# Tables, state matrices, modulation sums and convolution taps at other places in a written engine order

## The chip, the cores and the metric

The kernel runs on one core of one Trainium2 chip. The metric is the device time of one execution in microseconds (us); the figure for the kernel before is the median of three runs.

## The reference, cut to what is computed

Two token streams of 128 tokens and width 1024 (a prompt and a sample) pass through the same two layers. Every layer has three branches (a convolution of 31 taps, a state space model run in both directions, and attention), which are merged by gates and added to the stream. All arithmetic is float32.

```python
def _layer(x, mods, lp, angles, ctx_k, ctx_v, init_re, init_im):
    shift, scale, gate = mods                       # _adaln(c, w_ada, b_ada): silu(c) @ w + b
    h = _rmsnorm(x, lp['norm_g']) * (1.0 + scale) + shift
    z = h @ lp['w_in']
    conv_in, conv_gate, ssm_in, ssm_gate, q, k, v, attn_gate, merge = jnp.split(z, cuts, axis=-1)
    ya = _conformer_conv(conv_in, ...)              # a*sigmoid(g), 31 taps, layer norm, silu
    br_a = (ya * jax.nn.silu(conv_gate)) @ lp['w_conv_out']
    yb, fin_re, fin_im = _s5_bidirectional(ssm_in, ...)
    yg_a, yg_b = jnp.split(jax.nn.gelu(yb) @ lp['w_ssm_glu'], 2, axis=-1)
    br_b = (yg_a * jax.nn.sigmoid(yg_b) * jax.nn.silu(ssm_gate)) @ lp['w_ssm_out']
    ...
    br_c = (_blocked_attention(q, k_all, v_all) * jax.nn.silu(attn_gate)) @ lp['w_attn_out']
    mixed = g_a * br_a + g_b * br_b + g_c * br_c
    return x + gate * (mixed @ lp['w_out']), side
```

In the state space model `lam_bar = exp(lam*dt)`, `b_bar = ((lam_bar-1)/lam) * b`, and the state follows `h[t] = lam_bar*h[t-1] + b_bar u[t]` per group (32 groups, 64 complex states, 16 channels).

## The kernel before, in words

**One order, five engines.** `stages()` and `order(l)` (L56 and L126) write out one list of stages. Every engine walks the same list and does its own share of each stage, waiting on semaphores; so the place of a stage in the list sets what an engine does before and after it, and an instruction that waits holds up all that stands behind it on its engine. SyncE (SP) issues the weight loads in the list's order into seven slots (`raw`, `RAW` = 7, 512 KB each), and a slot is loaded again when its slab has been read.

**Split products.** The units `cg`, `ssm`, `ca` (L40) and all merge (`me`), branch (`br`) and output (`wo`) products are done as three products of rounded parts (L826 to L828). For each piece of weights (two k tiles) ScalarE writes the high part (`high_parts`, L1163) into one of a few rooms (five `early_room`, three `late_room`), and VectorE subtracts it for the low part (`low_parts`, L1466). TensorE waits for the low part (L821). `ahead(l, u, beside)` (L446) says how many pieces of the next unit are split beside a unit's own, two as a rule. The other units (`q`, `kv`, `sg`, `ag`, `gg`, `glub`, `glua`) are plain float32 products (L798).

**The opening.** The layer norm, the modulation (`ada`, `adaE`, `adaT`) and `hT` give the scaled input; `early` splits it. `tabA`, `tabS`, `tabB`, `tabC` make the tables of powers of lam (VectorE, with ScalarE for `tabS`). `bT` and `cT` transpose the state matrices b and c. `pre` (L1759) multiplies b by powers of lam in halves of 16 groups, six VectorE operations each, into the one buffer `pre`; `preE` transposes it on TensorE (`states_in`, L834) and ScalarE copies it to `E`. `pre` of the second half waits until the first has been transposed (L1764). `bbar` (L1746) scales b itself.

**The state space part.** `pack` and `UT` bring the tokens into groups (`Uz`). `S` (L938) multiplies E by Uz: eight banks of four products, each bank copied by ScalarE (partitions 0 to 63, L1342) and VectorE (64 to 127, L1743) into `H`. In the kernel before, the product writes its bank with the chunk number outermost, so both copies read the bank in a row and write runs of 16 values. `cp` (L1780) needs tA and tB and, here, `bbar`; `bz` on GpSimd needs `bbar`; `K` on TensorE needs `cp` and `bz`. `scan` runs 32 steps of four VectorE operations, `qkn` normalises q and k, `Y` reads the states back (`HY`, L1409 on ScalarE and L1881 on VectorE).

**Convolution taps.** A layer has 124 tap operations on VectorE (L1570), dealt out by hand: 4 ahead of `Y`, 18 in it, 25 in `att` 0, 20 in `att` 1, 14 beside each of the two B combinations, and the rest (29) in `("conv", -1, "C0")`, behind which `cback` waits.

**End of a layer.** `comb` A mixes the last branch; `pre` of the next layer stands as a block between; `wout` multiplies by w_out, `wx` (`out_and_add`, L1588) adds to x; `sq` and `xn` normalise for the next layer.

Side banks in PSUM are a ring of three, claimed in the list's order (`Ring`, L211).

## Time and profile before

| | kernel before |
|---|---|
| median of three runs (lowest to highest) | 738.4 us (738.39 to 740.62) |
| the profiled execution: time, and its span from first to last instruction | 741.45 us, 739.4 us |
| mean granted TensorE clock in that span | 0.962 |
| busy: TensorE, VectorE, ScalarE, GpSimd | 656.6, 546.4, 291.3, 35.4 us |
| weight loads | 16 DMA engines busy about half of the span, 117.65 MB |

The span is what the rows below count in, from its first instruction; the time is 2.05 us longer than the span, and the profiled execution is 3.05 us above the median. A row of the timeline gives start, duration, engine, line, operation, tile written and tiles read, how often, and in brackets the idle time of the engine ahead of it and what ended it. A granted clock of 1.00 is 2.4 GHz, 0.50 is 1.2 GHz.

### The profile page before, as it was taken

Reading aid. Unit: us, or ns where it says so; the run is one execution under the profiler, and the core shown is the slowest. Engines: PE = TensorE matmul, PEld = TensorE weight load, DVE = VectorE, ACT = ScalarE, POOL = GpSimd, SP = SyncE. Lnnn points to the kernel's source line nnn. Section 1 sums busy time; section 2 is a strip of 40 time slices with the busy share of each in tenths; the row PEclk is TensorE's granted clock in tenths of the full one; section 3 lists DMA queues with packets and bytes.
Section 4 is the critical chain, followed back from the end, with each engine's and each line's share of the span. In section 5 each row is a group of like instructions: output and inputs, shape, how many; then the busy total and the mean of one; then the engine's idle time right before and its main releaser. Section 6 shows DMA issues by size and latency. Waiting matters only on the chain.

```text
span 739.4 us, 9579 instructions
## 1 busy us (share of the span) xinstructions
PE 656.6 (89%) x3573; PEld 473.0 (64%) x3573; DVE 546.4 (74%) x1024; ACT 291.3 (39%) x454; POOL 35.4 (5%) x49
## 2 busy tenths in 40 slices
PE   3669679999898999987898797999898999989997
PEld 1357574653744688775787686665485568867885
DVE  3873769994757988988767444899778699897564
ACT  2454322211535454442544642311254345434541
POOL 2100010102000000010000001001200000000000
PEclk9979789999999999998999998999999999999999
DMA  8973623862675365544433347281254236655531
GB/s 283 355 204 97 204 71 118 281 225 57 208 230 173 100 218 165 176 132 124 144 122 105 113 150 274 81 293 54 55 195 121 81 95 194 189 153 151 192 121 57
DMA packets 67305, 117.65 MB, mean 159 GB/s; under 512 B 11052, under 2 KB 15484, under 8 KB 67260
## 3 DMA queue, kind: packets, MB, share of 16 engines
q1 hardware_dynamic: 66980, 116.94, 49.8%
q8 instruction: 28, 0.46, 0.3%
q14 instruction: 17, 0.14, 0.1%
q10 hardware_dynamic: 280, 0.11, 0.1%
HBM read 112.51 MB, written 1.38 MB: 154 GB/s over the span
## 4 chain that ended last, share of the span: by engine, by line
PE 71%; DVE 20%; issue 3%; ACT 3%; SPq 1%; DMA 0%; POOL 0%; ACTq 0%; POOLq 0%; DVEq 0%
PE proj L798 20%; PE proj L826 11%; PE proj L827 11%; PE proj L828 11%; DVE cvacc L1570 4%; PE side L813 3%; DVE raw_split L1463 3%; PE side L951 3%; PE side L965 2%; PE side L1044 2%; PE long L768 2%; PE side L994 2%; DVE tA L1463 1%; DVE tB L1463 1%; PE side L1042 1%
## 5 line engine op out<-in xcount | busy, mean ns | idle before, releaser
L798 PE MATMUL proj<-raw,hT 128*128 128x512 f32 (+1 forms) x320 | 132.0, 558 | 0.0
L1570 DVE SCALAR_TENSOR_TENSOR cvacc<-cvpad,taps,cvacc 128x256 f32<-128x256 f32 x240 | 99.2, 478 | 0.3
L798 PEld LDWEIGHTS proj<-raw,hT 128*128 128x128 f32 x320 | 58.2, 190 | 58.8 <-issue 57.0
L1179 ACT ACTIVATE wide_split<-raw 128x1024 fp32r<-128x1024 f32 x56 | 58.6, 1059 | 58.0 <-PE proj L828 53.2
L1463 DVE TENSOR_TENSOR raw_split<-raw,wide_split 128x1024 fp32r<-128x1024 f32 x56 | 67.6, 1220 | 18.6 <-ACT wide_split L1179 17.6
L827 PE MATMUL proj<-raw_split,H_split 128*128 128x512 f32 x192 | 76.6, 399 | 0.0
L826 PE MATMUL proj<-wide_split,H_split 128*128 128x512 f32 x144 | 59.4, 412 | 12.8 <-DVE raw_split L1463 12.5
L828 PE MATMUL proj<-wide_split,H_split 128*128 128x512 f32 x144 | 58.0, 403 | 0.0
L1463 DVE TENSOR_TENSOR raw_split<-raw,utok_split 128x1024 fp32r<-128x1024 f32 x28 | 34.2, 1221 | 12.6 <-ACT utok_split L1179 12.5
L1179 ACT ACTIVATE utok_split<-raw 128x1024 fp32r<-128x1024 f32 x28 | 29.6, 1058 | 35.1 <-PE proj L828 35.1
L827 PEld LDWEIGHTS proj<-raw_split,H_split 128*128 128x128 f32 x192 | 37.2, 194 | 7.3
L826 PEld LDWEIGHTS proj<-wide_split,H_split 128*128 128x128 f32 x144 | 27.9, 193 | 21.1 <-DVE raw_split L1463 13.1
L1463 DVE TENSOR_TENSOR H<-H,qkt 128x128 f32<-128x128 f32 x128 | 38.4, 300 | 2.2
L827 PE MATMUL proj<-raw_split,mixed_split 128*128 128x512 f32 x96 | 39.1, 407 | 0.0
L827 PE MATMUL proj<-raw_split,qM_split 128*128 128x512 f32 x96 | 37.7, 393 | 0.0
L828 PEld LDWEIGHTS proj<-wide_split,H_split 128*128 128x128 f32 x144 | 28.1, 195 | 6.3
L813 PE MATMUL side<-ident,pre 128*128 128x128 f32 x128 | 19.9, 293 | 11.0 <-DVE pre L1463 7.5
L798 PE MATMUL proj<-raw,HY 128*128 128x512 f32 x64 | 29.0, 596 | 0.0
L1376 ACT ACTIVATE pre<-side,nmx 128x128 f32<-128x128 f32 (+1 forms) x32 | 13.2, 416 | 39.7 <-PE side L813 16.4
L1152 ACT ACTIVATE gates<-proj 128x512 f32<-128x512 f32 x12 | 7.0, 597 | 54.7 <-PE proj L798 54.7
L951 PE MATMUL side<-Uz,EC 128*128 128x128 f32 x128 | 20.5, 340 | 8.9 <-DVE Uz L1736 8.9
L813 PEld LDWEIGHTS side<-ident,pre 128*128 128x128 f32 x128 | 16.6, 152 | 18.1 <-DVE pre L1463 7.7
(251 smaller groups left out, 1336.9 us busy)
## 6 DMA issues: line engine op xcount, KB each, us to landing
raw<-in_w_in SPq DMA_DIRECT2D x104, 512.0 KB, 4.2
raw<-in_w_ada SPq DMA_DIRECT2D x48, 512.0 KB, 5.1
...
```

The source lines that it names most:

```text
L768: m = T.matmul(ring.bank(part)[rows_, 0:ADA_W], cond[:, kt, :], w[:, j // 2, ADA_W * (j % 2):ADA_W * (j % 2) + ADA_W], start=(kt == 0), st ...
L798: m = T.matmul(proj.bank((l, u, s))[:, 0:n], lhs[:, s, kt, :], w[:, i, :], start=(kt == 0), stop=last)
L813: return T.transpose(out, in_, ident[0:k, 0:k])
L826: T.matmul(bank[:, :], hi, whi, start=(kt == 0), stop=False)
L827: T.matmul(bank[:, :], hi, wlo, start=False, stop=False)
L828: m = T.matmul(bank[:, :], lo, whi, start=False, stop=last)
L951: m = T.matmul(out[:, gg, r, :, :, :], E[:, r, gp, :], Uz[:, 2 * gp:2 * gp + 2, :].rearrange("p a (s k) -> p a s k", s=NS), start=True, st ...
L965: m = T.matmul(side.bank(key)[0:48, 80 * b:80 * b + 80], bz[:, r, g % 16, :], CP[:, r, :, g, :], start=(r == 0), stop=(r == 1))
L994: T.matmul(side.bank(key)[:, 0:2 * nk * P], qT[:, s, p, :], kz[s][:, :, :].rearrange("p a k -> p (a k)"), start=True, stop=True).then_inc( ...
L1179: S.activation(piece_room[m], piece_raw(m), ACT.Copy).then_inc(piece_hi, 1)
L1463: return V.tensor_tensor(out, a, b, op)
L1570: m = V.scalar_tensor_tensor(acc, src, taps[:, t, j:j + 1], acc, ALU.mult, ALU.add)
```

## The change

- The opening of layer 0: `tabB` moves from ahead of `early` to behind the unit `cg`; `cT` moves ahead of the unit `ssm`, and c is loaded right behind b; the first `preE` moves behind `ca` and the taps. `pre` of the second half goes to a buffer of its own (`first_pre`, in the room of `H` that held `xn`), so it no longer waits for the first half's transposes. `cg` now splits four pieces of `ssm` beside its own.
- `bbar`: in layer 0 behind `cp`, in layer 1 between `ssm` and `ca` (before: ahead of `UT` in both).
- `S`: the products write the bank with the chunk number innermost, the copies read the bank in a row and write single values 512 bytes apart.
- `adaT` (modulation sums) behind `Y`; `qkT` 1 ahead of `att` 0; taps dealt out anew: 16 or 8 ahead of `Y` (layer 0, 1), 40 or 30 in `att` 0, 22 in `att` 1, 12 beside each B combination, so 4 or 22 remain for `C0`.
- `pre` of layer 1, first half, behind the transposes of branch A, and both halves with low parts of the A units between their six operations (`upto`).
- The edge of the layers: the three low parts of the next `cg` behind the first `wx`; `preE` of the second half cut in two on ScalarE with `sq` between; the first `hT` transposes inside the last product of w_out (`tokens_t`); the second `wx` behind the first `early`.

```diff
+TAPS_IN_ZONE = (16, 8)
+TAPS_IN_ATT = (((8, 8, 8, 8, 8), (7, 4, 4, 7, 0)), ((6, 6, 6, 6, 6), (7, 4, 4, 7, 0)))
...
-    begin = [("unit", "cg"), ("tabC",), ("bT", 0), ("unit", "ssm"), ("cT", 0), ("pre", 0, 0), ("preE", 0, 0),
-             ("chunks", "ca", 4), ("pre", 0, 1), ("unit", "ca"), ("taps", 0), ("pack",), ("preE", 0, 1)]
+    begin = [("unit", "cg"), ("tabB",), ("tabC",), ("bT", 0), ("cT", 0), ("unit", "ssm"), ("pre", 0, 0),
+             ("chunks", "ca", 4), ("pre", 0, 1), ("unit", "ca"), ("taps", 0), ("preE", 0, 0), ("pack",), ("preE", 0, 1)]
     if l:
-        begin = [("hT", 0, 0), ("hT", 1, 0), ("early", 0, 0), ("sq", l, 1), ("early", 1, 0), ("xn", l, 1),
+        begin = [("hT", 0, 0), ("hT", 1, 0), ("early", 0, 0), ("wx", l - 1, 1), ("early", 1, 0), ("sq", l, 1), ("xn", l, 1),
-                 ("unit", "ca"), ("pack",)]
+                 ("bbar", l), ("unit", "ca"), ("pack",)]
+    turn = [] if l else [("bbar", l)]
     return (begin
-            + [("bbar", l), ("bz", 0), ("UT",), ("S",), ("cp",), ("convT", 0), ("convT", 1), ("unit", "q"), ("unit", "kv"),
+            + [("UT",), ("S",), ("cp",)] + turn + [("bz", 0), ("convT", 0), ("convT", 1), ("unit", "q"), ("unit", "kv"),
-            + [("scan", 0, NCHUNK), ("qkn",), ("adaT", l, 2)] + nxt("adaT", n, 0)
-            + [("conv", 4, None), ("Y",), ("qkT", 0), ("att", 0)] + nxt("adaE", n, 1)
-            + [("geT",), ("qkT", 1), ("att", 1), ("unit", "glub"), ("unit", "glua"), ("split", 0), ("split", 1)]
+            + [("scan", 0, NCHUNK), ("qkn",), ("conv", TAPS_IN_ZONE[l], None), ("Y",), ("adaT", l, 2)] + nxt("adaT", n, 0)
+            + [("qkT", 0), ("qkT", 1), ("att", 0)] + nxt("adaE", n, 1)
+            + [("geT",), ("att", 1), ("unit", "glub"), ("unit", "glua"), ("split", 0), ("split", 1)]
-            + [("brT", "B", 0), ("brT", "B", 1), ("conv", 14, "B0"), ("comb", "B", 0)]
-            + nxt("bT", n) + [("brT", "C", 0), ("brT", "C", 1), ("conv", 14, "B1"), ("comb", "B", 1)]
+            + [("brT", "B", 0), ("brT", "B", 1), ("conv", 12, "B0"), ("comb", "B", 0)]
+            + nxt("bT", n) + [("brT", "C", 0), ("brT", "C", 1), ("conv", 12, "B1"), ("comb", "B", 1)]
-            + nxt("taps", n) + [("cback", 0), ("cback", 1), ("comb", "C", 1)] + nxt("pre", n, 0)
-            + [("brT", "A", 0), ("brT", "A", 1), ("comb", "A", 0)] + nxt("preE", n, 0) + nxt("pre", n, 1)
-            + [("comb", "A", 1), ("wout", 0), ("wout", 1), ("wx", 0)] + nxt("sq", n, 0) + nxt("preE", n, 1)
-            + nxt("xn", n, 0) + [("wx", 1)])
+            + nxt("taps", n) + [("cback", 0), ("cback", 1), ("comb", "C", 1)]
+            + [("brT", "A", 0), ("brT", "A", 1)] + nxt("pre", n, 0) + [("comb", "A", 0)] + nxt("preE", n, 0)
+            + nxt("pre", n, 1) + [("comb", "A", 1), ("wout", 0), ("wout", 1), ("wx", l, 0)] + nxt("preE", n, 1)
+            + nxt("sq", n, 0) + nxt("preF", n, 1) + (nxt("xn", n, 0) or [("wx", l, 1)]))
...
-                            ("tabS",), ("hT", 0, 0), ("hT", 0, 1), ("tabB",), ("early", 0, 0), ("early", 0, 1),
+                            ("tabS",), ("hT", 0, 0), ("hT", 0, 1), ("early", 0, 0), ("early", 0, 1),
...
+        first_pre = H[:, :, :].rearrange("p a b -> p (a b)")[:, 0:2048].rearrange("p (r g j c) -> p r g j c", r=2, g=16, j=L)
+        pre_of = lambda ll, half: first_pre if (ll, half) == (0, 1) else pre
...
+                    sp.wait_ge(bbar_done, l)
...
+                    c_loads(0)
-                    c_loads(0)
...
+            def tokens_t(l, h, s):
+                pe.wait_ge(xn_second if h else xn_first, ls(l, s))
+                key = ("hT", l, h, s)
+                side.claim(pe, key)
+                for i in range(4):
+                    d = 4 * h + i
+                    m = transpose(side.bank(key)[:, P * i:P * i + P], xn[:, s, P * d:P * d + P])
+                m.then_inc(side.full, 1)
...
-                                          pre[:, r, g:g + 2, :, :].rearrange("p g j c -> p (g j c)"))
+                                          pre_of(ll, half)[:, r, g:g + 2, :, :].rearrange("p g j c -> p (g j c)"))
...
-                    pe.wait_ge(xn_second if h else xn_first, ls(l, s))
-                    key = ("hT", l, h, s)
-                    side.claim(pe, key)
-                    for i in range(4):
-                        d = 4 * h + i
-                        m = transpose(side.bank(key)[:, P * i:P * i + P], xn[:, s, P * d:P * d + P])
-                    m.then_inc(side.full, 1)
+                    if l == 0 or s:
+                        tokens_t(l, h, s)
...
-                        out = side.bank(key)[:, :].rearrange("p (k g a r s) -> p g r a s k", k=NCHUNK, g=2, a=2, r=2)
+                        out = side.bank(key)[:, :].rearrange("p (g a r q) -> p g r a q", g=2, a=2, r=2)
-                                m = T.matmul(out[:, gg, r, :, :, :], E[:, r, gp, :],
-                                             Uz[:, 2 * gp:2 * gp + 2, :].rearrange("p a (s k) -> p a s k", s=NS),
+                                m = T.matmul(out[:, gg, r, :, :], E[:, r, gp, :], Uz[:, 2 * gp:2 * gp + 2, :],
...
+                                    if s == 1 and kt == 5 and l + 1 < DEPTH:
+                                        for h in range(2):
+                                            tokens_t(l + 1, h, 0)
...
-                elif k == "preE":
+                elif k in ("preE", "preF"):
-                    for r in range(2):
+                    for r in ((0,) if stg == ("preE", l + 1, 1) else (1,) if k == "preF" else range(2)):
...
-                    high_parts(ahead(l, "cg"))
+                    high_parts(ahead(l, "cg", 4))
...
-                        S.activation(H[0:64, 1:NCHUNK + 1, 16 * i:16 * i + 16],
-                                     side.bank(key)[0:64, :].rearrange("p (k x) -> p k x", k=NCHUNK),
+                        dst = H[0:64, 1:NCHUNK + 1, 16 * i:16 * i + 16].rearrange("p k x -> p x k")
+                        S.activation(dst, side.bank(key)[0:64, :].rearrange("p (x k) -> p x k", k=NCHUNK),
...
-                    low_parts(ahead(l, stg[1]))
+                    low_parts(ahead(l, stg[1], 4 if stg[1] == "cg" else 2))
...
-                        V.tensor_copy(H[64:128, 1:NCHUNK + 1, 16 * i:16 * i + 16][:, ::-1, :],
-                                      side.bank(key)[64:128, :].rearrange("p (k x) -> p k x", k=NCHUNK)
+                        dst = H[64:128, 1:NCHUNK + 1, 16 * i:16 * i + 16][:, ::-1, :].rearrange("p k x -> p x k")
+                        V.tensor_copy(dst, side.bank(key)[64:128, :].rearrange("p (x k) -> p x k", k=NCHUNK)
                 elif k == "bbar":
+                    if ll == 0:
+                        dve.wait_ge(cp_done, 2)
...
-                    side.filled(dve, ("E", ll, 3) if half else ("cT", ll, 1))
+                    if half == 0:
+                        side.filled(dve, ("cT", ll, 1))
+                    elif ll:
+                        side.filled(dve, ("E", ll, 3))
+                    else:
+                        for h, s in itertools.product(range(2), range(NS)):
+                            side.filled(dve, ("hT", ll, h, s))
+                        dve.wait_ge(pre_done, 1)
+                    upto = lambda i: low_parts(piece_at[(l, f"meA{half}", 0)] + i) if ll else None
+                        upto(3 * r + 1)
+                        upto(3 * r + 2)
+                        upto(3 * r + 3)
-                        m = tt_(pre[:, r, :, :, :], t1, t2, ALU.add if r else ALU.subtract)
+                        m = tt_(pre_of(ll, half)[:, r, :, :, :], t1, t2, ALU.add if r else ALU.subtract)
...
-                    dve.wait_ge(bbar_done, l + 1)
+                    if l:
+                        dve.wait_ge(bbar_done, l + 1)
...
-                        else:
-                            for _ in range(5):
-                                conv_tap(*taps_left.pop(0))
+                        for _ in range(TAPS_IN_ATT[l][s][p]):
+                            conv_tap(*taps_left.pop(0))
...
+                        low_parts(piece_at[(l, "wo1", 3)] + 1)
+                elif k == "wx":
+                    out_and_add(stg[1], 1, stg[2])
+                    if stg[2] == 0:
-                elif k == "wx":
-                    out_and_add(l, 1, stg[1])

```

## Rows read from the trace of the kernel before

**Rows 1.** Page, part 1: busy us, share of the span and instructions, by engine.

```profile
PE 656.6 (89%) x3573; PEld 473.0 (64%) x3573; DVE 546.4 (74%) x1024; ACT 291.3 (39%) x454; POOL 35.4 (5%) x49
```

**Rows 2.** TensorE's waits: engine, line waited for: us in all, times, longest us.

```profile
PE proj L826 <- DVE raw_split L1463: 22.3, 10, 8.4
...
PE side L813 <- DVE cvacc L1570: 2.5, 2, 1.8
```

**Rows 3.** Windows: stretch, length, busy us (count) by engine, clock, DMA share, GB/s.

```profile
42.80:48.00 5.20, 5.19 (x13) 4.11 (x14) 5.01 (x5) 2.92 (x4) 0.00 (x0) 0.51 0.36 133
...
48.00:56.00 8.00, 8.00 (x36) 6.53 (x35) 4.41 (x13) 2.54 (x3) 0.00 (x0) 1.00 0.91 219
...
103.20:108.70 5.50, 5.48 (x26) 5.50 (x27) 1.39 (x2) 1.18 (x2) 1.85 (x4) 0.50 0.00 0
```

**Rows 4.** Timeline of the opening: sums' transposes, sums, first split product.

```profile
33.10 0.44 PE L813 MATMUL side<-ident,adarow 128*128 128x128 f32 x2 [0.51 <-ACT adarow L1202]
...
37.77 0.23 DVE L1463 TENSOR_TENSOR ada<-side,modc 128x8 f32<-128x8 f32 x2
...
42.81 0.77 PE L826 MATMUL proj<-gates_split,mixed_split 128*128 128x512 f32 x1 [8.41 <-DVE raw_split L1463]
```

**Rows 5.** Windows: tabB, tabC, pre half, bbar, cp, scan with qkn, S to Y.

```profile
29.27:36.55 7.28, 4.50 (x54) 2.19 (x42) 6.56 (x23) 2.90 (x7) 0.00 (x0) 1.00 0.93 327
...
50.47:53.80 3.33, 3.33 (x16) 2.69 (x16) 3.26 (x13) 0.12 (x1) 0.00 (x0) 1.00 1.25 279
...
72.62:79.91 7.29, 0.00 (x0) 0.00 (x0) 7.17 (x6) 0.61 (x2) 0.00 (x0) 0.67 0.43 143
...
97.96:101.79 3.83, 1.09 (x16) 0.96 (x16) 3.79 (x6) 1.77 (x4) 0.00 (x0) 1.00 0.18 70
...
114.25:128.75 14.50, 14.50 (x55) 5.69 (x54) 14.25 (x12) 1.81 (x4) 0.00 (x0) 1.00 0.43 135
...
128.76:176.33 47.57, 47.57 (x303) 26.05 (x302) 42.41 (x144) 8.79 (x26) 7.49 (x7) 1.00 0.65 216
...
113.49:183.66 70.17, 70.17 (x394) 35.10 (x392) 57.37 (x156) 12.46 (x32) 7.49 (x7) 1.00 0.55 179
```

**Rows 6.** Copies by line: ns min/median/max, first and last start, form.

```profile
L1342 ACT ACTIVATE H<-side x16: 591/591/592, 105.3 to 468.5; 64x512 f32<-64x512 f32 x16
...
L1743 DVE COPY H<-side x16: 694/695/696, 105.3 to 468.5; 64x512 f32<-64x512 f32 x16
...
L1229 ACT ACTIVATE bbar<-side x4: 1032/1051/1054, 58.6 to 275.6; 128x512 f32<-128x512 f32 x4
...
L1881 DVE COPY HY<-H x8: 1023/1048/1070, 186.6 to 544.2; 64x1024 f32<-64x1024 f32 x8
```

**Rows 7.** Timeline ahead of S in layer 0.

```profile
79.95 3.68 PE L813 MATMUL side<-ident,pre 128*128 128x128 f32 x16 [7.46 <-DVE pre L1463]
...
93.56 1.23 DVE L1463 TENSOR_TENSOR pre<-tA,tB 128x1024 f32<-128x1024 f32 x1
...
103.22 10.28 PE L951 MATMUL side<-Uz,EC 128*128 128x128 f32 x64 [4.16 <-DVE Uz L1736]
```

**Rows 8.** Timeline at the start of attention of stream 1, layer 0.

```profile
225.01 2.06 DVE L1570 SCALAR_TENSOR_TENSOR cvacc<-cvpad,taps,cvacc 128x256 f32<-128x256 f32 x5
...
229.20 1.10 PE L994 MATMUL side<-kz,qM 128*128 128x512 f32 x2 [1.82 <-DVE kz L1830]
```

**Rows 9.** Timeline at the start of Y in layer 0.

```profile
184.07 3.78 ACT L1409 ACTIVATE HY<-H 64x1024 f32<-64x1024 f32 x2
...
187.78 0.43 PE L1042 MATMUL side<-qM,Uz 128*64 128x64 f32 x2 [3.12 <-DVE HY L1881]
```

**Rows 10.** Timeline in the A combination of layer 0.

```profile
347.10 0.80 PE L826 MATMUL proj<-wide_split,H_split 128*128 128x512 f32 x1 [5.09 <-DVE raw_split L1463]
```

**Rows 11.** Timeline at the edge of the layers.

```profile
417.83 0.47 PE L826 MATMUL proj<-gates_split,mixed_split 128*128 128x512 f32 x1 [2.69 <-issue]
```

**Rows 12.** Timeline at the start of S in layer 1.

```profile
458.25 2.05 PE L951 MATMUL side<-Uz,EC 128*128 128x128 f32 x8 [4.76 <-DVE Uz L1736]
```

## The prediction, made before the changed kernel was run

> **What bounds the kernel now.** I read the page first: TensorE is busy 656.6 of 739.4 us [rows 1], so all that a new order can win is its 82.8 us of idling and what the clock costs beside it. Then TensorE's waits: VectorE ends most of them, the low parts of split weights alone ten waits of 22.3 us, the last taps of a layer two of 2.5 [rows 2]. Then the windows around such waits: after the wait ahead of 42.8 the granted clock is 0.51 (the 1.2 GHz level) and 13 products take 5.2 us, then it is 1.00 and 36 take 8.0, so a product is 0.40 or 0.23 us; the bank products of S begin at 0.50 as well [rows 3]. I count nine waits with such a stretch behind or around them. So TensorE is the bound nearly everywhere, and the question at each moved stage is whether VectorE still ends a wait there.
>
> **The opening of layer 0.** The modulation sums run on VectorE at 37.77, though TensorE's transposes for them are done at 33.54; the first split product starts at 42.81 after a wait of 8.41 [rows 4]. In between VectorE does `tabB`, to 36.55 [rows 5]. With `tabB` gone the sums move up by 4.2, and with them the second half of `hT`, `early` and the first low part: first product at about 38.8. Then I follow VectorE. TensorE reads the first `cg` piece (12 products, cold, 5.2) until 44.0 and the third until 49.5 (24 more at 0.23); only then the fourth `ssm` piece has a room. ScalarE's copy of 1024 columns, from its 0.59 for 512 [rows 6], is 1.1, and a low part costs VectorE what one of the six equal operations of a half of `pre` costs (7.29/6 = 1.2 [rows 5]): ready at 51.9. Behind it stand on VectorE `tabB` 7.28, `tabC` 3.33, four low parts of `ca` 4.8, two halves of `pre` 14.6 [rows 5], together 30.0, without a wait among them that I can find: 81.9. TensorE meanwhile has `cg` to 52, some 5 for b and c and 48 products each of `ssm` and `ca` at 0.23, so until about 79, and the wait of 7.46 for `pre` [rows 7] goes and VectorE is late by some 3 only at the end. From the last `pre` (94.79) to the first product of S (103.22) it took 8.4 [rows 7]; 3.8 of that was `bbar` [rows 5], now behind `cp`. The copy of `pack` comes into that line, as it now stands on ScalarE behind the first `preE`; 0 to 1.9, I take 0.8. S then starts at 81.9 + 8.4 - 3.8 + 0.8 = 87.3 instead of 103.2: **-15.9**. Bounds: -17 without the `pack`, -8 if some link of this chain of thirty steps costs twice what it should. On SP the four loads of c now pass three `ssm` loads; those pieces wait for rooms, which covers some 3 us of delay.
>
> **The copies of S.** ScalarE will write values 512 bytes apart. Its nearest row, 512 columns written 64 bytes apart, takes 1.05 us against 0.59 for the copy of now; VectorE's nearest row, 1024 values read 512 bytes apart, takes 1.05 us, no more per value than its S copy of now with 0.695 for 512 [rows 6]. So I take 1.05 on ScalarE and 0.7 on VectorE, with 1.25 (VectorE by ScalarE's factor 1.8) as the other bound and no gain possible on either. With three banks TensorE isn't held by 1.05; **+1.0** for both layers.
>
> Here the Trainium skill has a rule that speaks against the change: "Advanced Engine Details and Errata", SBUF Cachelines, says that accesses which go to another 16-byte line each time pay. For ScalarE the rows agree, for VectorE's reads they don't. By that rule VectorE's copies pay as well, the second rival below.
>
> **Scan to Y, layer 0.** VectorE becomes the bound. From the end of S (113.49) it needs about 0.7 to its last copy, 14.5 for `cp`, now 3.8 for `bbar`, 47.6 for scan and `qkn` [rows 5], 16 taps at 0.41 (five in 2.06 [rows 8]) and 1.05 for the first `HY`: 74.2. Now `Y` starts at 187.78, which is 74.3, after `adaT` had held VectorE [rows 9]. TensorE is done after 70.2 [rows 5] and ScalarE's `HY` some 2 later (two copies in 3.78 [rows 9]), so the wait stays: **-0.1**. In layer 1 (`bbar` earlier, 8 taps) the same sum ends at ScalarE's `HY`, about 0.6 early. GpSimd's `bz` waits for `bbar` but ends some 5 us before `K` needs it.
>
> **Attention.** `qkT` 1 goes ahead, so the 1.82 ahead of the first scores of stream 1 [rows 8] loses the cause that its row names; but these scores also wait until VectorE has read the sums of stream 0, and in front of that stand in layer 0 eight taps twice instead of five, 6 x 0.41 = 2.4 more. With `adaT` and `qkT` 1 ahead of the scores (1.5) and the `kz` copy saved, stream 1 starts 3.0 late; in stream 1 taps and slack cancel: **+3.0**. In layer 1 (six instead of five, one sum less) it is +0.6, which cancels the 0.6 above: **0**.
>
> **C combination.** Layer 0 has 4 taps left there instead of 29, so VectorE is 10 us ahead and the waits for the last taps and the low part behind them (2.6 together, in [rows 2]) go but for 0.5: **-2.1**. Layer 1 has 22 instead of 29, 2.9 less: of three waits of 4.5 there, 1.8 + 1.8 go: **-3.6**. The taps that filled this went to stages where, up to the two costs above, VectorE idled.
>
> **A combination.** TensorE waits 5.09 at 347.10 because the whole first `pre` (7.3) stands in front of a low part [rows 10]; a second such wait, for the second half, is 2.4 long. With low parts between the operations each costs 1.2 + 1.2 = 2.4, less than the 12 x 0.23 = 2.8 that TensorE takes for a piece. The lookahead ends inside the first three operations, so 1.5 of the first wait stays: 3.6 + 2.4 = **-6.0**. Bound -3: the first half misses its slot.
>
> **The edge.** The first product of layer 1 waits until 417.83, the last 2.69 for `hT` [rows 11]. With three low parts (3.6) behind `wx` x is ready 3.6 earlier, `sq` no longer holds `E` copies, and the transposes run inside the last product. The first product comes almost 5 earlier, but then the second stream's `hT` waits for the second `wx`, now behind `early`: I take **-2.9**, between 0 and -5.9 (both waits gone).
>
> **S, layer 1.** `bbar` leaves the line, its 3.8 of the wait of 4.76 [rows 12]: **-3.7**. VectorE idles between `ssm` and `ca`, where it goes.
>
> **Clock.** Where waits go, the stretches at 1.2 GHz behind them go: up to 2.7 us each for the two S stages (half of 5.5 [rows 3]), and, as half of the stretches that the granted clock shows, 4.4 in A (5.1 and 3.7 us) and 1.9 in C (3.8 us): 11.7. As waits of 1 to 4 us stay or come anew ahead of S, `Y` and stream 1, I take 7, less 0.9 for a longer wait ahead of `Y`: **-6.1**; bounds 0 and -11.
>
> **Sum.** -15.9 + 1.0 - 0.1 + 3.0 - 2.1 - 3.6 - 6.0 - 2.9 - 3.7 - 6.1 = -36.4 us on the profiled 741.45 (span 739.4, 2.05 around it), so 705.0 in such an execution. That one lay 3.05 above the median 738.4, so the forecast for a median is **702.0**. Its own range is 694 to 710 (the clock's bounds and some 3 us of the opening).
>
> **The rivals.**
> - The copies of S cost VectorE 1.25 each. Eight copies then take 4.4 longer, of which S's own pace hides some 1.5, and as VectorE sets the start of `Y` in both layers, 2.9 each come onto the path, and 1.1 each on S: 702 + 8 = **710**. For it: ScalarE's row. Against it: VectorE's strided reads. This is the result that the Trainium skill's rule on 16-byte lines ("Advanced Engine Details and Errata", SBUF Cachelines) would give.
> - The opening gives half: VectorE's chain of thirty steps meets a wait (the fourth `ssm` piece, for which VectorE waits ahead of all tables), so S starts at 95 instead of 87: 702 + 8, and some 6 more when the first half in A also misses its slot: **716**. For it: nothing on VectorE can pass a late low part. Against: no other link shows a wait.
> - Clock and edge give their full bounds: 702 - 5 - 3 = **694**.
> - Slower than before: the single-value writes into `H` stop being a rate of one value per cycle on VectorE, and its chain through S, `cp` and scan, which has no slack in either layer, takes it all. 16 copies must add 36.4 + 2.2 us, so it decides from 2.4 us more per copy, 3.1 instead of 0.7; at 3.5 each the time is **747**. ScalarE's factor of 1.8 is far below that, no row has more.
> - The change doesn't do what it says: tables moved behind `cg` just stall later. With the opening at 0 and the rest kept: **718**.
>
> **How the numbers follow.** Forecast 0.55; copies 0.18; half an opening 0.12; full bounds 0.06; nothing in the opening 0.03; slower 0.04; no change, by several of these at once, 0.02. The range takes the forecast's own band, the copies and half an opening: 692 to 719. A difference of 0.3% (2.2 us) is about what a measurement of this kernel can tell from no change. Faster 0.94, same 0.02, slower 0.04.
>
> **What the changed profile would show.** The first split product near 38.8; S near 87, with no `bbar` ahead of it; VectorE's S copies at 0.7 and ScalarE's near 1.05; `Y` 74 us behind the end of S, with VectorE as releaser; scores of stream 1 late behind the taps; no wait above 2 us in the A combination; the start of layer 1 some 3 us sooner behind the last product of w_out; S of layer 1 within 1.2 us of the transposes of U. I am wrong if VectorE's copies take over 1 us, if S starts after 92, or if waits of 3 us and more appear where none were.

## The result and the profile after

The changed kernel takes 714.4 us (median of four, 713.0 to 715.4) beside 738.8 for the kernel before on the same chip: a ratio of 0.966, 95% interval 0.964 to 0.969, so 24.4 us faster. Compared once more with the kernel before, it took 713.1 beside 739.6 (0.963, 0.960 to 0.966). The forecast was 702.0 with a range of 692 to 719: the direction and the range held, the gain was two thirds of what was forecast. The profiled execution after took 713.04 with a span of 711.0; the one before took 741.45 with 739.4. Trace against trace 28.4 us went.

The page after: busy times by engine, and the granted TensorE clock in 40 slices.

```profile
PE 652.4 (92%) x3573; PEld 466.5 (66%) x3573; DVE 551.5 (78%) x1024; ACT 297.3 (42%) x454; POOL 36.4 (5%) x49
...
PEclk9989889998998999999999999999998999999999
```

TensorE is busy 4.2 us less than in [rows 1], in a span 28.4 shorter: what went is mostly its idling (82.8 us before, 58.6 now). The waits of TensorE after, as who waited for whom: total, times, longest.

```profile
PE proj L833 <- DVE raw_split L1477: 11.3, 10, 4.2
PE side L1053 <- DVE HY L1908: 8.4, 2, 5.4
...
PE side L1005 <- DVE qkt L1477: 4.5, 2, 2.7
...
PE long L1022 <- DVE pre L1882: 2.9, 2, 1.7
...
PE side L820 <- DVE taps L1629: 2.0, 1, 2.0
```

The low parts cost 11.3 where they cost 22.3 in [rows 2], and the waits for the last taps are gone from the list. What stands out now are the waits ahead of Y (HY), two kinds in the attention (qkt, pre) and one for the copy of the taps.

Where the 28.4 us lie, by the start of the same instruction in both traces (the starts of before that the prediction used are in [rows 4, 7 to 9, 11, 12], the rest is read from its trace in the same way):

| stage | before | after | change | forecast |
|---|---|---|---|---|
| start to S, layer 0 | 103.2 | 90.1 | -13.1 | -15.9 |
| S, layer 0 | 10.3 | 9.1 | -1.2 | in copies and clock |
| end of S to Y, layer 0 | 74.3 | 75.7 | +1.4 | -0.1 |
| Y to the first split product behind the attention, layer 0 | 67.3 | 72.0 | +4.7 | +3.0 |
| from there to the transposes of cvacc | 56.2 | 56.9 | +0.7 | 0 |
| C combination, layer 0 | 21.5 | 19.4 | -2.1 | -2.1 |
| A combination, layer 0 | 54.6 | 44.6 | -10.0 | -6.0 and clock |
| w_out and edge to S, layer 1 | 70.9 | 64.6 | -6.3 | -6.6 |
| S, layer 1 | 10.3 | 7.4 | -2.9 | in copies and clock |
| end of S to Y, layer 1 | 67.6 | 67.5 | -0.1 | 0 |
| Y to the first split product, layer 1 | 63.6 | 66.7 | +3.1 | 0 |
| the rest | 139.7 | 137.0 | -2.7 | -3.6 |
| copies of S, clock, over all stages | | | in the rows above | +1.0, -6.1 |
| sum | | | -28.4 | -36.4 |

Three places carry the miss. First the opening. TensorE after, from the first transposes of `pre` that wait to S (start, duration, tile, count, wait and what ended it):

```profile
82.18 1.09 PE L820 MATMUL side<-ident,pre 128*128 128x128 f32 x8 [1.99 <-DVE taps L1629]
...
86.28 1.11 PE L820 MATMUL side<-ident,H 128*128 128x128 f32 x4 [0.77 <-ACT EC L1258]
...
90.12 9.10 PE L963 MATMUL side<-Uz,EC 128*128 128x128 f32 x64 [0.83 <-DVE Uz L1750]
```

VectorE in the same stretch:

```profile
79.50 1.22 DVE L1477 TENSOR_TENSOR H<-tA,tB 128x1024 f32<-128x1024 f32 x1
80.65 1.28 DVE L1740 SCALAR_TENSOR_TENSOR mixed<-th,proj 128x512 f32<-128x512 f32 x2
81.84 0.28 DVE L1629 COPY taps<-side 128x128 f32<-128x128 f32 x1
```

VectorE's chain ended at 80.7, even before the forecast 81.9. But eight transposes of the first half of `pre`, which VectorE had finished at 71.3, stood behind the copy of the taps, whose bank they want, and VectorE reached that copy only behind everything else.

Then the attentions. TensorE after, ahead of stream 1 in layers 0 and 1:

```profile
214.59 0.66 PE L1022 MATMUL long<-v,pre 128*128 128x64 f32 x4 [1.20 <-DVE pre L1882]
...
218.80 2.04 PE L1005 MATMUL side<-kz,qM 128*128 128x512 f32 x2 [2.67 <-DVE qkt L1477]
220.64 4.99 PE L805 MATMUL proj<-raw,HY 128*128 128x512 f32 x8
...
541.91 0.66 PE L1022 MATMUL long<-v,pre 128*128 128x64 f32 x4 [1.71 <-DVE pre L1882]
...
545.32 2.05 PE L1005 MATMUL side<-kz,qM 128*128 128x512 f32 x2 [1.87 <-DVE qkt L1477]
547.16 5.56 PE L805 MATMUL proj<-raw,HY 128*128 128x512 f32 x8
```

In layer 0 a late start was forecast: the two waits are 3.87 together where they were 1.98 before. In layer 1 they are 3.58 where they were 3.13, so there the terms nearly cancelled, as forecast. Not foreseen was what stands behind them in both layers: two scores take 2.04 and 2.05, the eight products with `HY` 4.99 and 5.56. In the trace of before they took 1.10 and 3.60 in both layers. Layer 1 of before:

```profile
569.82 0.66 PE L1011 MATMUL long<-v,pre 128*128 128x64 f32 x4 [1.31 <-DVE pre L1854]
...
573.87 1.10 PE L994 MATMUL side<-kz,qM 128*128 128x512 f32 x2 [1.82 <-DVE kz L1830]
574.80 3.60 PE L798 MATMUL proj<-raw,HY 128*128 128x512 f32 x8
```

The windows after show the granted clock of those stretches (the column behind POOL's):

```profile
219.00:225.00 6.00, 6.00 (x9) 2.48 (x10) 3.89 (x10) 2.30 (x5) 0.00 (x0) 0.63 0.19 47
...
545.30:551.00 5.70, 5.68 (x7) 2.51 (x8) 3.98 (x10) 2.30 (x5) 0.00 (x0) 0.50 0.00 1
```

The third place is the start of Y, where TensorE waits 5.44 us in layer 0, and the miss of 1.5 there.

### The profile page after: what moved, and what is told of

The parts are those of the page before. It is cut to its first block and busy times, and to the rows that moved or that the text cites. A ratio compares the mean times of both kernels' runs of the same rounds, so it can differ in the third digit from the quotient of the medians.

```text
span 711.0 us, 9584 instructions
## 1 busy us (share of the span) xinstructions
PE 652.4 (92%) x3573; PEld 466.5 (66%) x3573; DVE 551.5 (78%) x1024; ACT 297.3 (42%) x454; POOL 36.4 (5%) x49
## 5 line engine op out<-in xcount | busy, mean ns | idle before, releaser
L1477 DVE TENSOR_TENSOR raw_split<-raw,wide_split 128x1024 fp32r<-128x1024 f32 x56 | 67.9, 1220 | 21.6 <-ACT wide_split L1193 20.9
L1193 ACT ACTIVATE wide_split<-raw 128x1024 fp32r<-128x1024 f32 x56 | 58.6, 1059 | 55.9 <-PE proj L835 55.9
L833 PE MATMUL proj<-wide_split,H_split 128*128 128x512 f32 x144 | 57.9, 402 | 4.7 <-DVE raw_split L1477 4.7
L835 PE MATMUL proj<-wide_split,H_split 128*128 128x512 f32 x144 | 56.9, 395 | 0.0
L834 PEld LDWEIGHTS proj<-raw_split,H_split 128*128 128x128 f32 x192 | 36.4, 190 | 7.3
L834 PE MATMUL proj<-raw_split,mixed_split 128*128 128x512 f32 x96 | 38.5, 401 | 0.0
L805 PE MATMUL proj<-raw,HY 128*128 128x512 f32 x64 | 32.4, 653 | 0.0
L1053 PE MATMUL side<-qM,Uz 128*64 128x64 f32 x128 | 19.7, 239 | 8.4 <-DVE HY L1908 8.4
L1055 PE MATMUL side<-EC,HY 128*64 128x64 f32 x256 | 25.4, 237 | 0.0
L834 PE MATMUL proj<-raw_split,HY_split 128*128 128x512 f32 x64 | 24.9, 390 | 0.0
```

The source lines that it names most:

```text
L805: m = T.matmul(proj.bank((l, u, s))[:, 0:n], lhs[:, s, kt, :], w[:, i, :], start=(kt == 0), stop=last)
L833: T.matmul(bank[:, :], hi, whi, start=(kt == 0), stop=False)
L834: T.matmul(bank[:, :], hi, wlo, start=False, stop=False)
L835: m = T.matmul(bank[:, :], lo, whi, start=False, stop=last)
L1053: T.matmul(o, Uz[:, g, :], M[:, :, g // 2, :], start=True, stop=False)
L1055: m = T.matmul(o, HY[:, q % 2, gi, r, :, :].rearrange("p s k -> p (s k)"), CP[:, r, 1:L + 1, g, :], start=False, stop=(r == 1))
```

## The experiments

Each kernel is the changed one with the edit shown, if nothing else is said. Times are medians of four, ratios are to the kernel before on the same chip, and traces are compared with that of the changed kernel (span 711.0).

| kernel | us | ratio, 95% interval | span of the trace |
|---|---|---|---|
| changed | 714.4 | 0.966 (0.964 to 0.969) | 711.0 |
| changed, once more | 713.1 | 0.963 (0.960 to 0.966) | 711.3 |
| S in the layout of before | 712.0 | 0.962 (0.961 to 0.964) | 710.5 |
| attention taps dealt anew | 707.1 | 0.954 (0.949 to 0.958) | 704.7 |
| no taps ahead of Y | 711.9 | 0.960 (0.957 to 0.964) | 709.9 |
| copy of the taps later | 711.1 | 0.961 (0.959 to 0.962) | 708.7 |
| tables back | 714.9 | 0.965 (0.962 to 0.968) | 713.0 |
| pre in one piece | 722.0 | 0.975 (0.971 to 0.978) | 720.7 |
| edge back | 719.6 | 0.972 (0.968 to 0.976) | 716.6 |
| all taps dealt as before | 704.6 | 0.953 (0.951 to 0.954) | 703.3 |
| bbar back ahead of S | 714.5 | 0.966 (0.964 to 0.968) | 711.1 |
| combined | 692.8 | 0.936 (0.931 to 0.942) | 692.4 |
| combined, HY early | 692.2 | 0.936 (0.935 to 0.938) | 688.5 |

### The measure: the changed kernel once more

> The changed kernel once more, nothing altered, on the chip and beside the runs of the other three. It is the measure for small differences. Theory: its stages differ from the first trace of it only where the granted clock fell or did not fall behind the same waits (S of layer 0, the start of Y, the first split products of layer 0), so 713 to 716, and each stage without such a stretch within 0.2 us. Rival: the first profiled execution (713.0) was a different case from the others, with other waits.

713.1 us, the same waits at the same places: 5.47 ahead of Y, 1.20 and 2.66, 1.70 and 1.88 ahead of stream 1. Stage by stage the traces differ by up to 0.3 us, and by 0.5 ahead of S of layer 0 and 0.4 in it (9.51 against 9.10). So a stage of one trace is good to some 0.3 us where the clock is steady. The start of S in layer 0 scatters more: in the eight traces here whose order is the same up to there it lies between 89.6 and 91.0. The two medians of this kernel differ by 1.2 us; differences of less than 2 us are read below from the traces, not from the medians.

### The copies of S

```diff
-    out = side.bank(key)[:, :].rearrange("p (g a r q) -> p g r a q", g=2, a=2, r=2)
+    out = side.bank(key)[:, :].rearrange("p (k g a r s) -> p g r a s k", k=NCHUNK, g=2, a=2, r=2)
...
-    dst = H[64:128, 1:NCHUNK + 1, 16 * i:16 * i + 16][:, ::-1, :].rearrange("p k x -> p x k")
-    V.tensor_copy(dst, side.bank(key)[64:128, :].rearrange("p (x k) -> p x k", k=NCHUNK)
+    V.tensor_copy(H[64:128, 1:NCHUNK + 1, 16 * i:16 * i + 16][:, ::-1, :],
+                  side.bank(key)[64:128, :].rearrange("p (k x) -> p k x", k=NCHUNK)
```

> The changed kernel with the S stage alone back in the layout of before (chunk outermost). In the changed kernel's trace VectorE's eight copies of S follow one another at 0.92 us with no idle time, in the kernel before they took 0.69 and stood 0.89 apart, which is TensorE's own rate for a bank at full clock. Theory: the new layout costs 0.22 us a copy, and as TensorE needs 0.89 a bank anyway, only about 0.25 us of each S stage and 0.25 of each last copy reach the path: this kernel is 1 us faster than the changed one (time 713.4 against 714.4, the profile's S of layer 1 7.1 long against 7.38, Y of layer 0 starting 0.5 sooner behind the start of S). Rival: the layout shortened S (10.26 to 9.1 and 7.4 us in the two layers), so taking it back costs 1 to 3 us a layer, up to 720.

VectorE's copies of S, first in the changed kernel, then in this one (shortest, median, longest in ns):

```profile
L1758 DVE COPY H<-side x16: 1031/1048/1053, 92.2 to 439.9; 64x512 f32<-64x512 f32 x16
```

```profile
L1758 DVE COPY H<-side x16: 694/695/696, 92.5 to 439.5; 64x512 f32<-64x512 f32 x16
```

A copy takes 1.05 us on VectorE, not 0.7, and as long on ScalarE. But in either layout the copies of S in layer 1 start 0.89 apart, which is TensorE's pace for a bank at full clock; the longer ones overlap. So S of layer 1 takes 7.38 us in either layout, and from its start to VectorE's last copy it is 8.49 against 8.11: the layout costs 0.4 us a layer, all of it in the last copy. The theory was right on the size (0.8 for both layers, 1.0 expected), but not on its place, as S itself was to fall to 7.1. The rival, that the layout had shortened S, fell: with the layout of before S of layer 1 takes 7.38 here, so the 10.3 of before were its low clock.

### The attention's taps

```diff
-TAPS_IN_ATT = (((8, 8, 8, 8, 8), (7, 4, 4, 7, 0)), ((6, 6, 6, 6, 6), (7, 4, 4, 7, 0)))
+TAPS_IN_ATT = (((9, 9, 9, 4, 3), (11, 4, 4, 7, 0)), ((7, 7, 8, 2, 1), (11, 4, 4, 7, 0)))
```

> The changed kernel with the taps of the attention dealt in another way: stream 0 gets 9,9,9,4,3 instead of 8,8,8,8,8 (layer 0) and 7,7,8,2,1 instead of 6,6,6,6,6 (layer 1), stream 1 gets 11,4,4,7,0 instead of 7,4,4,7,0, the rest (none in layer 0, one tap in layer 1) goes to the C combination. Theory: the taps of the last two steps hold the copy of the probabilities and the sums of stream 0, so the waits of 1.20 and 2.67 us (layer 0) and 1.71 and 1.87 (layer 1) ahead of stream 1 go but for 0.3 each, and with them the granted clock's fall behind them: the first piece with HY takes 3.6 us again instead of 4.99 and 5.56, the first scores 1.1 instead of 2.05, and the first split products of layer 0 gain 1.5. Together some 12 us, 702 us. Rival: VectorE is the bound of the whole attention, so the same taps make the same waits at other steps: 0 to 3 us, 711 to 714. Second rival: the clock's fall has nothing to do with these waits but with the transposes of q and k that no longer stand there: waits gone, clock still low, 707.

TensorE in this kernel, ahead of stream 1 of layer 0:

```profile
216.70 1.10 PE L1005 MATMUL side<-kz,qM 128*128 128x512 f32 x2 [0.69 <-DVE qkt L1477]
217.63 3.60 PE L805 MATMUL proj<-raw,HY 128*128 128x512 f32 x8
```

The wait is 0.69 instead of 2.67, the other is gone, and scores and products are back at 1.10 and 3.60. The same in layer 1 (0.35, 1.10). With the transposes of q and k still moved, the clock stays up once the taps no longer hold VectorE, so the second rival, in which those transposes alone bring the clock down, falls. From Y to the first split product it is 67.6 and 61.7 instead of 72.0 and 66.7. The expected 12 us were not all there, though: VectorE, now later at the end of stream 1, makes TensorE wait 0.89 and 0.52 for its last copy of the probabilities, the first split products of layer 0 run at a granted clock of 0.60 and those of layer 1 at 0.75, and in the C combination of layer 1, with one tap more, a wait grows from 1.28 to 1.69. Of 12 us 7 came (6.3 by the trace).

### The taps ahead of Y

```diff
-TAPS_IN_ZONE = (16, 8)
+TAPS_IN_ZONE = (0, 0)
...
-            + [("brT", "B", 0), ("brT", "B", 1), ("conv", 12, "B0"), ("comb", "B", 0)]
+            + [("brT", "B", 0), ("brT", "B", 1), ("conv", 14, "B0"), ("comb", "B", 0)]
```

(and 14 for B1.)

> The changed kernel without the 16 (layer 0) and 8 (layer 1) taps between the normalisation of q and k and the copies for Y; the B combination takes 14 and 14 instead of 12 and 12, the C combination the rest (12 and 4 more). Theory: VectorE sets the start of Y only because these taps (6.35 and 3.3 us) stand in front of its first copy for Y; TensorE is done 5.4 and 3.0 us earlier. The wait of 5.44 falls to about 1, the one of 2.98 to about 0.5, and the slow products at the start of Y (pairs of 1.06 instead of 0.70 us in layer 0) gain 2; the C combination gives back 1 to 3. 6 us faster than the changed kernel, 708. Rival: the taps come due at the C combination in any case, and the gain is paid back there by waits for the last taps of 4 to 5 us and for the low parts behind them: 713 to 716.

Inconclusive as to the time (1.2 us and 2.5 us below the two medians of the changed kernel), clear as to what is late next. TensorE at the start of Y, layer 0:

```profile
172.92 0.30 PE L1053 MATMUL side<-qM,Uz 128*64 128x64 f32 x2 [2.62 <-DMA qM<-wide]
```

Without the 16 taps VectorE is out of the way and Y starts 72.9 us behind the end of S instead of 75.7, but then the transfers that write `qM` are the ones it waits for. In layer 1, where ScalarE's copy ends the wait now (2.74), it gains only 0.25, and layer 1 loses 3.1 between the attention and the A combination. Theory and rival are each right in part: in layer 0 the wait falls, though to 2.62 and not to 1, and in layer 1 the gain is paid back.

### The copy of the taps

```diff
-             ("chunks", "ca", 4), ("pre", 0, 1), ("unit", "ca"), ("taps", 0), ("preE", 0, 0), ("pack",), ("preE", 0, 1)]
+             ("chunks", "ca", 4), ("pre", 0, 1), ("unit", "ca"), ("preE", 0, 0), ("pack",), ("preE", 0, 1), ("taps", 0)]
```

> The changed kernel with one stage of layer 0 moved: the transposes and the copy of the taps stand behind the last transposes of pre, not ahead of the first. Theory: half of the miss at the start of S (90.1 instead of 87.3) is that TensorE's second eight transposes of pre wait 1.99 us for a bank that VectorE's copy of the taps frees, and VectorE comes to that copy only behind the whole second half of pre and the two operations of the ca unit. Without it TensorE goes on at 80, and ScalarE's copies with it: S starts at 88.1, 2 us sooner; 712.4. Rival: in that stretch ScalarE is the bound (eight copies of 0.54, the pack of 1.90, two of 0.59), and S starts within 0.5 us of 90.1: 714.

TensorE ahead of S in this kernel:

```profile
84.59 0.66 PE L820 MATMUL side<-ident,H 128*128 128x128 f32 x4 [1.46 <-ACT EC L1258]
...
87.83 9.01 PE L963 MATMUL side<-Uz,EC 128*128 128x128 f32 x64 [1.01 <-DVE Uz L1750]
```

S at 87.8, 2.3 sooner, and all 2.3 arrive at the end (span 708.7). Theory right; with the scatter of the start of S, this is 1.8 us or more of the 2.8 that the opening missed.

### The tables of VectorE

```diff
-    begin = [("unit", "cg"), ("tabB",), ("tabC",), ("bT", 0), ("cT", 0), ("unit", "ssm"), ("pre", 0, 0),
+    begin = [("unit", "cg"), ("tabC",), ("bT", 0), ("cT", 0), ("unit", "ssm"), ("pre", 0, 0),
...
-                            ("tabS",), ("hT", 0, 0), ("hT", 0, 1), ("early", 0, 0), ("early", 0, 1),
+                            ("tabS",), ("hT", 0, 0), ("hT", 0, 1), ("tabB",), ("early", 0, 0), ("early", 0, 1),
```

> The changed kernel with the tables of VectorE (tabB, 7.28 us) alone back at their old place, ahead of the modulation sums of the second half. Theory: their move is what brought the start of S forward, so S starts 4.2 later again, at 94 instead of 90.1, and the time is 718.5. Rival: the move only hands the 7.28 us on. The first split product goes back to 42.8, but VectorE's chain behind the fourth ssm piece is 7.3 shorter, so VectorE is no longer late there; TensorE, 4 us later, sets the start of S itself: within 1.5 of 90.1, and 713 to 716.

TensorE at the first split product and at S:

```profile
42.86 0.77 PE L833 MATMUL proj<-gates_split,mixed_split 128*128 128x512 f32 x1 [8.21 <-DVE raw_split L1477]
...
92.02 9.01 PE L963 MATMUL side<-Uz,EC 128*128 128x128 f32 x64 [1.01 <-DVE Uz L1750]
```

The first split product goes back 4.4 us, to where it was in [rows 4], yet S starts only 1.9 later, and the wait for the copy of the taps is gone, because VectorE, 7.3 lighter, is no longer late. Between the two, nearer to the rival: the move of the tables is worth some 2 us at S (1.0 to 2.4, with the scatter of that start), not 4; the medians differ by 0.5 and 1.7. With the tables back, 11.2 of the opening's 13.1 us are still there. What the second buffer for `pre`, the later `preE` and the four pieces of `ssm` each give of them, no run separates.

### bbar of layer 0

```diff
-             ("taps", 0), ("preE", 0, 0), ("pack",), ("preE", 0, 1)]
+             ("taps", 0), ("preE", 0, 0), ("pack",), ("preE", 0, 1), ("bbar", 0)]
...
-    turn = [] if l else [("bbar", l)]
+    turn = []
```

> The changed kernel with bbar of layer 0 (3.83 us on VectorE) back ahead of S, the rest as it is. By the prediction's step its move is 3.8 of the gain ahead of S, so this kernel is 3.8 slower, 718. Rival: VectorE sets the start of Y, and bbar is on its line on either side of S; S starts 3.4 us later, but from the end of S to Y it takes 3.8 less and GpSimd's bz, which follows bbar, no longer runs beside the scan (steps of 1.36 instead of 0.61), so TensorE's wait of 5.4 ahead of Y shrinks to about 1, Y starts within 1 us of where it did, and the time is 712 to 715.

TensorE at S and at the start of Y, layer 0:

```profile
92.82 9.95 PE L963 MATMUL side<-Uz,EC 128*128 128x128 f32 x64 [3.74 <-DVE Uz L1750]
...
175.62 0.30 PE L1053 MATMUL side<-qM,Uz 128*64 128x64 f32 x2 [2.59 <-DMA qM<-wide]
```

The rival, but for one point: S starts 2.7 later, Y 0.7 later, the median is 714.5 and the span 711.1. The wait ahead of Y does not shrink to 1, though: 2.59 stay, behind the transfers that write `qM`. VectorE is no longer the one that Y waits for. Moving `bbar` behind `cp` gained next to nothing, as VectorE has to do it before Y on either side of S.

### The A combination

```diff
-                    upto = lambda i: low_parts(piece_at[(l, f"meA{half}", 0)] + i) if ll else None
+                    upto = lambda i: None
```

> The changed kernel with each half of pre of layer 1 in one piece on VectorE in the A combination of layer 0, no low part between its operations, all else as it is. Theory: the low parts between them are the gain there, so a wait of 4 to 5 us and one of 2.4 come back with the slow stretches behind them, and the combination (323.2 to 367.9) is 8 to 10 us longer: 723. Rival: the first wait went because VectorE comes to A earlier, with 4 taps left for the C combination instead of 29: then at most 3 us come back, 717.

TensorE's waits in the A combination of layer 0:

```profile
338.08 0.80 PE L833 MATMUL proj<-wide_split,H_split 128*128 128x512 f32 x1 [5.19 <-DVE raw_split L1477]
...
361.88 0.50 PE L833 MATMUL proj<-wide_split,H_split 128*128 128x512 f32 x1 [2.43 <-DVE raw_split L1477]
```

The window behind the first of them, with the granted clock at 0.56:

```profile
338.00:344.00 6.00, 5.92 (x16) 4.70 (x17) 2.29 (x3) 1.09 (x3) 0.00 (x0) 0.56 0.00 0
```

Both waits are back (5.09 in [rows 10]); the combination takes 53.3 instead of 44.6, the kernel 722.0. The rival fell: coming to A with fewer taps behind it does nothing for VectorE there, it is the low parts between the operations of `pre`.

### The edge

The second `wx` again right behind the first `xn`, the three low parts ahead of the first `wx`, `sq` of the first stream ahead of both copies of the second half of `E` and that of the second stream ahead of its `early`, the transposes of x of stream 0 behind the last product (the diff in part):

```diff
-            + nxt("pre", n, 1) + [("comb", "A", 1), ("wout", 0), ("wout", 1), ("wx", l, 0)] + nxt("preE", n, 1)
-            + nxt("sq", n, 0) + nxt("preF", n, 1) + (nxt("xn", n, 0) or [("wx", l, 1)]))
+            + nxt("pre", n, 1) + [("comb", "A", 1), ("wout", 0), ("wout", 1), ("wx", l, 0)] + nxt("sq", n, 0)
+            + nxt("preE", n, 1) + nxt("xn", n, 0) + [("wx", l, 1)])
...
-                                    if s == 1 and kt == 5 and l + 1 < DEPTH:
-                                        for h in range(2):
-                                            tokens_t(l + 1, h, 0)
```

> The changed kernel with the edge between the layers as before: both halves of wx of layer 0 behind the first xn, three low parts ahead of them, both squares one after the other, the transposes of x behind the last product, both copies of the second half of E together. Theory: the edge is worth 2.5 to 2.9 us: the wait ahead of the first product of layer 1 goes from 1.2 to 4 or more, and the wait of 1.09 for the second stream goes away: 717. Rival: the first product comes earlier but the second stream is late by the same amount, so nothing is lost: 714 to 715.

TensorE's waits at the edge:

```profile
387.30 1.12 PE L820 MATMUL side<-ident,pre 128*128 128x128 f32 x4 [3.17 <-ACT EC L1254]
...
399.72 0.65 PE L833 MATMUL proj<-gates_split,mixed_split 128*128 128x512 f32 x1 [2.68 <-issue]
```

The windows behind each of them:

```profile
388.00:394.00 6.00, 6.00 (x18) 4.76 (x18) 0.26 (x1) 1.42 (x3) 0.00 (x0) 0.58 0.29 83
...
400.00:408.00 8.00, 8.00 (x33) 6.35 (x33) 4.71 (x9) 5.23 (x10) 0.66 (x2) 0.80 0.01 3
```

In the kernel before, whose waits there were 3.17 and 2.69, the window with the first of them:

```profile
383.00:417.80 34.80, 28.54 (x148) 23.16 (x147) 21.56 (x28) 17.45 (x28) 0.74 (x2) 1.00 0.41 131
```

From the last transposes of `mixed` to S of layer 1 it is 71.4 instead of 64.6: 6.8 us, more than either expected. Waits are 3.0 of it: 3.17 and 2.68 here, and 0.29, 1.20, 1.09 and 0.24 in the changed kernel. The rest, 3.7, goes with the clock, which fell to 0.58 and 0.80 behind those waits in this trace; in the kernel before it stayed at 1.00 behind the first and at 0.99 behind the second, between 417.8 and 458.2. So the order of the edge is worth the 3 us of the theory where the clock stays up, and more where it falls.

### All taps as before

```diff
-TAPS_IN_ZONE = (16, 8)
-TAPS_IN_ATT = (((8, 8, 8, 8, 8), (7, 4, 4, 7, 0)), ((6, 6, 6, 6, 6), (7, 4, 4, 7, 0)))
+TAPS_IN_ZONE = (4, 4)
+TAPS_IN_ATT = (((5, 5, 5, 5, 5), (5, 5, 5, 5, 0)),) * 2
```

(and 14 and 14 in the B combination.)

> The changed kernel with the taps dealt as in the kernel before: 4 ahead of the copies for Y, five in each step of the attention (none in the last step of stream 1), 14 and 14 in the B combination, 29 for the C combination in both layers. By the steps of the prediction the new deal gains 2.1 and 3.6 in the C combinations and loses 3.0 in the attention, so taking it back costs 2.7: 717. Rival, from the runs with taps taken away: ahead of Y 2.6 and in the two attentions some 2.4 and 1.2 of waits come off, and with luck the slow stretches behind them (2 to 6), against 1.1 to 3 given back in each C combination: 706 to 711.

704.6: the rival's direction and a little more than its gain (706 to 711), 8.5 to 9.7 us faster than the changed kernel. The changed kernel's new deal is a loss. By the stages of the two traces, taking it back gains 2.6 and 0.3 ahead of Y, 4.9 and 4.9 from Y to the split products behind the attention and 0.7 in those of layer 0, and costs 2.1 and 3.7 from there to the end of the C combinations: 13.4 against 5.8. TensorE at the places where it gains and loses:

```profile
213.59 1.10 PE L1005 MATMUL side<-kz,qM 128*128 128x512 f32 x2 [1.48 <-DVE qkt L1477]
214.53 3.60 PE L805 MATMUL proj<-raw,HY 128*128 128x512 f32 x8
...
295.66 1.09 PE L820 MATMUL side<-ident,cvacc 128*128 128x128 f32 x8 [0.69 <-DVE cvacc L1584]
...
615.57 1.09 PE L820 MATMUL side<-ident,cvacc 128*128 128x128 f32 x8 [1.76 <-DVE cvacc L1584]
```

Waits of 1.48 ahead of the scores in layer 0, of 1.30 and 1.48 in layer 1, did not bring the clock down here; 1.20 and 2.67, and 1.71 and 1.87, did in the changed kernel. All nine traces with the new deal of the attention's taps have the slow stretch in both layers; the four with another deal have it in neither.

### Together

S in its old layout, the copy of the taps late, and

```diff
+TAPS_IN_ZONE = (8, 6)
+TAPS_IN_ATT = (((9, 9, 9, 4, 3), (10, 4, 4, 4, 0)), ((7, 7, 8, 2, 1), (10, 4, 4, 4, 0)))
+TAPS_IN_Y = ((8, 6, 10), (8, 6, 10))
```

with 14 and 14 in the B combination.

> The changed kernel with what the first four runs showed put together: S in the layout of before (0.4 us a layer), the copy of the taps behind the last transposes of pre (2.3), the taps of the attention dealt as 9,9,9,4,3 and 10,4,4,4,0 (layer 0) and 7,7,8,2,1 and 10,4,4,4,0 (layer 1), 8 and 6 taps instead of 16 and 8 ahead of the copies for Y, 8, 6, 10 in Y instead of 6, 6, 6, and 14 and 14 in the B combination; what is left for the C combination is 9 and 19. Theory: the gains lie in different waits and add: 0.8 + 2.3 + 6.5 (attention) + 2.6 (start of Y in layer 0) = 12 us, 702 against 714. Rival: taps taken from one place only fill another, so the gain is that of the first two and half of the rest: 707.

692.8 us, a ratio of 0.936 (0.931 to 0.942), 21.6 less than the changed kernel and the fastest order tried but for the next, which measures the same. Its page:

```profile
span 692.4 us, 9584 instructions
...
PEclk9989999999999999999999999999999999999999
```

By the traces 18.6 us went: 3.2 ahead of S, 3.0 and 0.4 ahead of Y, 5.8 and 5.7 from Y to behind the attention, 1.5 in the split products behind the attention of layer 0, less 1.0 more between attention and A in layer 1; the rest is within 0.1. The gains add, as the theory said, but they are far more than its 12 us. Of the 6.6 more by the traces 5.0 are in the attention, where 6.5 was counted: what the attention run lost again behind it (waits of 0.89 and 0.52, slow split products in layer 0) does not come here. Which of the new counts does that, four taps instead of seven in the last step of stream 1 or those in Y, is not shown. Of the 3.2 ahead of S 0.9 lies within the scatter of that start.

### What is late next

On the combined kernel, ScalarE's first two copies for Y ahead of its gate:

```diff
                 elif k == "unit" and stg[1] in ("sg", "ag"):
+                    if stg[1] == "ag":
+                        act.wait_ge(scan_done, l + 1)
+                        for q in range(2):
+                            hy_front(q)
                     gate(l, stg[1])
```

> The combined kernel with ScalarE's first two copies for Y ahead of its gate of ag, in the 14 us in which it waits for TensorE. In the combined kernel they end the waits of 2.58 and 2.70 ahead of Y. Theory: another is late within 0.5 us: in layer 0 the transfers that write qM (they ended the wait of 2.62 in the run without taps ahead of Y), in layer 1 VectorE's own copies; both waits shrink by 0.5 at most, the time is that of the combined kernel less 0 to 1. Rival: ScalarE alone is late, both waits go, 5 us and the clock behind them, 686.

TensorE at the start of Y in both layers:

```profile
167.82 0.47 PE L1055 MATMUL side<-qM,Uz 128*64 128x64 f32 x2 [2.29 <-DMA qM<-wide]
...
491.87 0.30 PE L1055 MATMUL side<-qM,Uz 128*64 128x64 f32 x2 [1.93 <-DVE HY L1917]
```

The releasers are the expected ones: 2.58 becomes 2.29 behind the transfers, 2.70 becomes 1.93 behind VectorE (0.5 at most was expected), and the medians (692.2, 692.8) can't be told apart. The trace is 3.9 shorter, but 3.2 of that are S of layer 0 and the split products behind the attention of layer 1, which ran at full clock here and not in the combined kernel's trace, though their order is the same. Ahead of Y ScalarE, VectorE and the transfers arrive within a microsecond of one another.

## Why the prediction was right, and where it was off

In direction and range it was right, for the reason given: TensorE is the bound, VectorE ended most of its waits, and a new order took half of those for low parts away (22.3 to 11.3 us). That the number fell into the range is partly luck: the forecast's own band was 694 to 710, and 714.4 lies above it, in the part that was there for dear copies of S (710) and half an opening (716), neither of which came. The gain was 8.0 us short by the traces, and the time 12.4 above the forecast by the medians. The other 4.4 is the step from trace to median: the forecast took off the 3.05 by which the profiled execution of before lay above its median, and that of after lies 1.3 below its own.

Point by point:
- **Opening, -15.9: measured -13.1.** VectorE's chain was right (end at 80.7, forecast 81.9; first split product 38.5; forecast 38.8, though 42.81 less 4.2 is 38.6). The step that failed is "VectorE is late by some 3 only at the end": the copy of the taps, which is behind that chain, was not in the sum, although TensorE's transposes of `pre` want its bank. Moving it back gives 2.3 of the 2.8. Inside the sum two shares were smaller than they looked: the tables gave some 2 us instead of 4.2, and of `bbar`'s 3.8 the run with it back shows 2.7 at S, nearly all of which comes back as VectorE's time before Y, as the sum for Y (-0.1) had already counted.
- **Copies of S, +1.0: measured 0.8.** A mis-sized price and a right sum. VectorE's copy takes 1.05, not 0.7: I took its nearest row for reads far apart, and these are writes. "VectorE's copies over 1 us" was named as a sign of error, and the price is most of the way to the rival's 1.25, but the rival's 8 us did not follow, since the copies still start 0.89 apart, at TensorE's pace, and only the last one's length comes onto the path. The rule of the Trainium skill, "Advanced Engine Details and Errata", SBUF Cachelines (an access that goes to another 16-byte line each time pays), agrees here for VectorE's writes, 0.695 against 1.048 us.
- **Scan to Y, -0.1 in layer 0: measured +1.4.** The releaser was right. About 1.1 of it is a cost that I had put down as nothing: GpSimd's `bz` now runs beside the scan (below). Another 0.3 is the longer last copy of S, which has its term above.
- **Attention, +3.0 and 0: measured +4.7, with +0.7 behind it, and +3.1.** This is the largest step that failed. The late start of stream 1 was right in kind, but it was priced as a wait alone. The waits grew by 1.9 us in layer 0 and by 0.45 in layer 1. But behind waits of 1.20 and 2.67, and of 1.71 and 1.87, scores and the first products with `HY` ran in part at half the clock (0.63 and 0.50 in the windows above): 0.9 + 1.4 us in layer 0, 0.9 + 2.0 in layer 1. So the terms of layer 1 ("six instead of five, one sum less") did cancel nearly, and the 3.1 there is the slow stretch, which waits of 1.31 and 1.82 did not bring before. The clock term had taken 4.7 off what could be regained for waits that stay or come ahead of S, Y and stream 1 together; the two attentions alone took 5.2, and the split products behind the first 0.7 more than before.
- **C combination, -2.1 and -3.6: measured -2.1 and -2.7, or 2.1 and 3.7 when the deal is taken back.** Right in size, but paid for elsewhere: "the taps that filled this went to stages where VectorE idled" is the sentence that was wrong. Net the new deal costs 7.7 us by the traces.
- **A combination, -6.0 and its share of the clock: measured -10.0**, with the wait of 1.58 that was forecast at 1.5. Taking the low parts out again costs 8.7.
- **Edge and S of layer 1, -2.9 and -3.7: measured -6.3 together**, and right in both parts by the waits. S starts 1.02 behind the transposes of U, forecast within 1.2, where it was 4.76: 3.7 for `bbar`, though no run moves `bbar` of layer 1 alone. The waits of the edge, 3.17 and 2.69 before, came down by 3.0. Taken back, the edge alone costs 6.8, more than its bound of 5.9, which is those two waits, because in that trace the clock fell behind them.
- **Clock, -6.1.** It can't be read off alone. S of layer 1 got all of its 2.9, S of layer 0 only 1.2.
